# The last projection of a streaming encoder: begin with two tiles by column halves, weights in four buffers through ScalarE's queue

## What is computed

```python
h = rmsnorm(x, norm_w)
q, k, v, z_a, xbc, z_b, dt_raw, g_a, g_b = jnp.split(h @ w_in, split_points(SPLITS), axis=-1)
...
o_a = (attn * jax.nn.silu(z_a)) @ w_o_attn
o_b = y @ w_o_ssd
merged = jax.nn.sigmoid(g_a) * o_a + jax.nn.sigmoid(g_b) * o_b
x = x + (merged @ w_out).astype(x.dtype)
```

## Time and profile before

| | us |
|---|---|
| runs, median of 3 | 2492.91 (2492.88 to 2493.34) |
| profiled execution, its own time | 2494.7 |
| its span (first to last instruction) | 2493.0 |
| last stage, from SyncE's first issue to the end | 2269.0 to 2493.0 |
| TensorE matmul busy, whole span | 2349.9 (94%) |
| VectorE / ScalarE / GpSimd busy | 754.8 / 794.2 / 618.1 |
| mean granted TensorE clock | 0.970 |
| bytes moved by DMA | 250.10 MB, mean 100 GB/s |

### The profile page before, as it was taken

One profiled execution on the slowest core, in us unless ns is written; L12 is line 12 of the kernel. 1 busy time (PEld: TensorE's weight loads), 2 busy tenths in 40 slices (PEclk: granted clock), 3 DMA queues, 4 the chain that ended last, 5 costly groups with the idle time before them and its releaser, 6 DMA issues. The chain is left out here.

```text
span 2493.0 us, 35438 instructions
## 1 busy us (share of the span) xinstructions
PE 2349.9 (94%) x12807; PEld 2111.6 (85%) x12807; DVE 754.8 (30%) x1470; ACT 794.2 (32%) x1892; POOL 618.1 (25%) x547
## 2 busy tenths in 40 slices
PE   6999999999999999999999499999759999996999
PEld 5999999999999999999999478888547888774887
DVE  4211000024444000100000456555256566653221
ACT  5211112134444111221111355555235445432000
POOL 3110101101110111011010355555255665650000
PEclk9999999999999999999999699999969999997999
DMA  4411121211211212111118644444275656524432
GB/s 161 96 62 69 55 84 57 81 69 56 81 69 69 79 58 78 69 69 69 69 68 54 171 102 118 117 117 98 67 198 144 163 157 180 161 78 158 137 126 97
DMA packets 280002, 250.10 MB, mean 100 GB/s; under 512 B 74184, under 2 KB 257336, under 8 KB 272760
## 3 DMA queue, kind: packets, MB, share of 16 engines
q1 hardware_dynamic: 277832, 248.81, 34.8%
q10 hardware_dynamic: 2112, 0.53, 0.1%
HBM read 158.35 MB, written 90.95 MB: 100 GB/s over the span
## 5 line engine op out<-in xcount | busy, mean ns | idle before, releaser
L74 PE MATMUL acc<-h_hi,w_hi 128*128 128x424 f32 (+1 forms) x2280 | 811.0, 356 | 10.2 <-DVE h_lo L563 7.8
L75 PE MATMUL acc<-h_lo,w_hi 128*128 128x424 f32 (+1 forms) x2280 | 807.9, 354 | 0.0
L76 PE MATMUL acc<-h_hi,w_lo 128*128 128x424 f32 (+1 forms) x2280 | 807.9, 354 | 0.0
L74 PEld LDWEIGHTS acc<-h_hi,w_hi 128*128 128x128 f32 x2280 | 430.5, 189 | 24.5 <-DVE h_lo L563 8.6
L75 PEld LDWEIGHTS acc<-h_lo,w_hi 128*128 128x128 f32 x2280 | 431.1, 189 | 7.1
L76 PEld LDWEIGHTS acc<-h_hi,w_lo 128*128 128x128 f32 x2280 | 430.7, 189 | 7.1
L332 POOL TENSOR_TENSOR w_lo<-w_raw,w_hi 128x1024 fp32r<-128x1024 f32 x57 | 144.6, 2538 | 1130.6 <-ACT w_hi L374 1130.6
L399 ACT ACTIVATE row<-acc 128x424 f32<-128x424 f32 (+1 forms) x215 | 112.5, 523 | 825.3 <-PE acc L76 825.3
L599 DVE SCALAR_TENSOR_TENSOR conv_acc<-conv_in,conv_wb,conv_acc 128x424 f32<-128x424 f32 (+2 forms) x216 | 126.1, 585 | 380.9 <-ACT conv_acc L444 373.1
L74 PE MATMUL a_o_ps<-a_w_hi,a_at_hi 128*128 128x512 f32 (+1 forms) x272 | 117.7, 433 | 2.0 <-DVE a_branch L1294 2.0
L74 PE MATMUL s_o_ps<-s_w_hi,s_y_hi 128*128 128x512 f32 (+1 forms) x272 | 113.3, 416 | 5.9 <-ACT s_rows L1839 5.9
(11 more groups left out here) (215 smaller groups left out, 3049.6 us busy)
## 6 DMA issues: line engine op xcount, KB each, us to landing
proj<-row SPq DMA_DIRECT2D x56, 1056.0 KB, 4.0
w_raw<-in_w_in_dram SPq DMA_DIRECT2D x28, 1024.0 KB, 5.2
s_feat<-proj SPq DMA_DIRECT2D x16, 1280.0 KB, 7.9
s_acs_b<-acs_dram SPq DMA_DIRECT2D x16, 1024.0 KB, 7.3
a_q_diag<-proj SPq DMA_DIRECT2D x66, 128.0 KB, 4.4
a_z<-proj SPq DMA_DIRECT2D x16, 512.0 KB, 4.8
a_gate_t<-proj SPq DMA_DIRECT2D x16, 512.0 KB, 4.6
branch_rows<-a_branch SPq DMA_DIRECT2D x16, 512.0 KB, 3.2
```

Source lines behind the costliest of these rows:

```text
L74: pe.matmul(out, hi, whi, start=first, stop=False)
L75: pe.matmul(out, hi, wlo, start=False, stop=False)
L76: return pe.matmul(out, lo, whi, start=False, stop=last)
```

## The change

Only `project_out` changes.

- There are four raw weight buffers instead of two, and a semaphore for each. ScalarE's queue issues the four loads, before anything else on ScalarE, with no wait between them. SyncE issues rows 0, x 0, rows 1, x 1.
- ScalarE: four loads, high(0), high(1), four quarters' rounding, high(2), then as before from high(3). `high(2)` waits for three column halves' products instead of two.
- VectorE: low(0), low(1), four quarters' low parts, add_x(0), low(2), add_x(1), then as before.
- TensorE: turn(0), turn(1); wait for the low parts of both tiles; first column half of tile 0, of tile 1; second half of tile 0; turn(2); second half of tile 1; then step(2) as before, which begins with turn(3). The products' count for `add_x` follows that order.

The steps m = 0 and 1 are thus written out in this new order; step 2 and all later ones are unchanged. The diff, cut to its core:

```diff
-        w_raw = sb("w_raw", [P, 2, KT, D // 4])
+        w_raw = sb("w_raw", [P, 4, KT, D // 4])
...
-        w_loaded = [sem("w_loaded0"), sem("w_loaded1")]
+        w_loaded = [sem(f"w_loaded{q}") for q in range(4)]
...
         def steps(eng, step):
-            for m in range(3):
-                step(m, m % 2)
+            step(2, 0)
...
@@ sync
-            load_w(sp, 0)
             load(0, 0)
-            load_w(sp, 1)
             load(1, 1)
-            load_w(sp, 2)
-            load_w(sp, 3)
...
@@ scalar
+            def load_w(q):
+                act.dma_start(w_raw[:, q], io.w_out.rearrange("(k p) n -> p k n", p=P)[:, :, q * QUARTER:(q + 1) * QUARTER])\
+                    .then_inc(w_loaded[q], 16)
+            def high_w(q):
+                act.wait_ge(w_loaded[q], 16)
+                act.activation(w_hi[:, :, q * QUARTER:(q + 1) * QUARTER], w_raw[:, q], ACT.Copy)\
+                    .then_inc(S["w_hi_ready"], 1)
...
-                after(act, S["product_ready"], 2 * m - 2)
+                after(act, S["product_ready"], 3 if isinstance(m, int) and m == 2 else 2 * m - 2)
...
+            for q in range(4):
+                load_w(q)
             high(0, 0)
+            high(1, 1)
             for q in range(4):
-                high_w(act, q)
+                high_w(q)
+            high(2, 0)
...
@@ vector
+            def products(m, h):
+                if isinstance(m, int) and m < 2:
+                    return m + 1 + 2 * h
+                return 2 * m + h + 1
...
-                    dve.wait_ge(S["product_ready"], 2 * m + h + 1)
+                    dve.wait_ge(S["product_ready"], products(m, h))
...
             low(0, 0)
+            low(1, 1)
             for q in range(4):
-                low_w(dve, q)
+                low_w(q)
+            add_x(0, 0)
+            low(2, 0)
+            add_x(1, 1)
...
@@ tensor
             turn(0, 0)
+            turn(1, 1)
+            pe.wait_ge(S["lo_ready"], 4)
+            for h in range(2):
+                pe.wait_ge(S["w_lo_ready"], 2 * h + 2)
+                product(0, 0, h)
+                if h == 1:
+                    turn(2, 0)
+                product(1, 1, h)
```

More of the change, by code:

```diff
@@ L2204, in project_out @@
         stored = [sem("stored0"), sem("stored1")]
-        load_w, high_w, low_w = load_split_weights(io.w_out, w_raw, w_hi, w_lo, w_loaded,
-                                                   S["w_hi_ready"], S["w_lo_ready"])
+        QUARTER = D // 4
         block = ctx.enter_context(nc.Block())
         def steps(eng, step):
-            for m in range(3):
-                step(m, m % 2)
+            step(2, 0)
             with eng.Fori(0, (TILES - 4) // 2) as j:
@@ L2297, in low, with low_w @@
                         .then_inc(S["lo_ready"], 1)
+            def low_w(q):
+                n = slice(q * QUARTER, (q + 1) * QUARTER)
+                dve.wait_ge(w_loaded[q], 16)
+                dve.wait_ge(S["w_hi_ready"], q + 1)
+                dve.tensor_tensor(w_lo[:, :, n], w_raw[:, q], w_hi[:, :, n].bitcast(FP32), ALU.subtract)\
+                    .then_inc(S["w_lo_ready"], 1)
+            def products(m, h):
+                if isinstance(m, int) and m < 2:
+                    return m + 1 + 2 * h
+                return 2 * m + h + 1
             def add_x(m, slot):
@@ L2331, in turn, with product @@
                     mm.then_inc(S["turned"], 1)
+            def product(m, slot, h):
+                t = TokenTile(m)
+                n = slice(h * BANK, (h + 1) * BANK)
+                for k in range(KT):
+                    mm = split_matmul(pe, o_ps[0:t.n, slot, h, :], m_hi[:, slot, k, 0:t.n],
+                                      m_lo[:, slot, k, 0:t.n], w_hi[:, k, n], w_lo[:, k, n],
+                                      k == 0, k == KT - 1)
+                mm.then_inc(S["product_ready"], 1)
             pe.wait_ge(S["const"], 2)
             turn(0, 0)
+            turn(1, 1)
[6 more added lines that the diff above has]
+                product(1, 1, h)
             def step(m, slot):
@@ L2342, in step @@
                 for h in range(2):
-                    if isinstance(m, int) and m == 0:
-                        pe.wait_ge(S["w_lo_ready"], 2 * h + 2)
-                    n = slice(h * BANK, (h + 1) * BANK)
-                    for k in range(KT):
-                        mm = split_matmul(pe, o_ps[0:t.n, slot, h, :], m_hi[:, slot, k, 0:t.n],
-                                          m_lo[:, slot, k, 0:t.n], w_hi[:, k, n], w_lo[:, k, n],
-                                          k == 0, k == KT - 1)
-                    mm.then_inc(S["product_ready"], 1)
+                    product(m, slot, h)
             steps(pe, step)
```

## The result

The change makes the kernel slower: 2501.1 us (median of 7 runs, 2497.8 to 2505.5) against 2494.0 for the kernel before, also 7 runs. The ratio is 1.0029 with a 95% interval of 1.0019 to 1.0040, which is 7.1 us and clear of no change. The middle lies beyond the 0.2% that I took as the limit for slower, but the interval begins just inside it. I had forecast 2497.4 with a range up to 2500.6, and "within 0.2%" as the likeliest class. The sign of the working was right and its size was not.

A forecast was written before the change was run, and what follows sets the result against it. TensorE was taken to set the end, bound by a relay before its first product and one hole: +5.06 (later start) - 2.06 (hole) + 1.5 (rows of tile 3) = +4.5 us, giving a median of 2497.4, range 2494.3 to 2500.6.

The forecast's parts named there:

- hole of 2.06 us: TensorE's idle wait after tile 0's first half for the fourth weight quarter's split; forecast to go, -2.06 us.
- T: Moment when ScalarE is through its four load issues with tile 0 turned; forecast 2279.8, ends 2277.4 and 2282.4.
- in turn: Sharing rule for the two DMA queues: packets taken alternately; with 1570 weight packets moved, T = 2281.0.
- by bytes: Sharing rule for the two DMA queues: equal bytes each; with 1570 weight packets moved, T = 2278.6.
- The weights don't set it: Start of products: quarter two lands by 2284.4, before ScalarE comes to it at 2285.5.
- The second rival: ScalarE isn't held, issues some 0.7 us each; first product about 2288.2, +2.5 us in all, 2495.4; chance 0.20.
- From T to the first product: Turning, rounding and low parts of both tiles and weights before TensorE's first product: 10.4 us.
- the new wait: TensorE stands in `turn(3)` for rows of tile 3, whose load waits for `add_x(0)`; +1.5 us.
- The clock: TensorE's 1.2 GHz stretch after its first product, 5.26 us before; no change forecast, 0.8 us either way.
- The first rival: ScalarE's fourth issue held until the first two loads have left; T = 2282.4, +7.1 us, 2500.0; chance 0.22.
- The third rival: ScalarE held as forecast, but rows of tile 3 land in time for `turn(3)`; +3.0 us, 2495.9; chance 0.08.
- the fourth: Rival: first product no later than 2285.14 and no second wait; -2.1 us, 2490.8; chance 0.05.

The follow-up runs named there:

- Kernel 1: The kernel before with four raw weight buffers instead of two and nothing else; 2490.9 us, ratio to before 0.9986.
- kernel 2: The changed kernel with two buffers and SyncE's old order of loads, so only the tile order is new; 2498.8 us, ratio to before 1.0016.
- kernel 3: Kernel 1 with the four weight loads at the head of ScalarE's queue, old order of tiles; 2496.5 us, ratio to before 1.0008.
- kernel 5: The changed kernel with rows of tile 3 loaded ahead of x of tile 2 in SyncE's queue; 2498.9 us, ratio to before 1.0019.
- kernel 11: The changed kernel with SyncE silent after rows of tile 0 until all four weight loads have landed; one run, 2505.1 us.
- kernel 4: The changed kernel with weight loads three and four issued after the rounding of quarter two; 2496.0 us, ratio to before 1.0006.
- kernel 10: The changed kernel with the edits of kernel 4 and kernel 5 together; 2495.2 us, ratio to before 1.0002.
- kernel 12: The changed kernel with each 1 MB weight load in 512 packets of 2 KB; 2495.9 us, ratio to before 1.0010.
- kernel 9: The changed kernel measured once more, unaltered; 2500.1 us, ratio to before 1.0023.
- kernel 7: Kernel 1 with SyncE's loads in order of need: rows 0, w0, w1, rows 1, w2, w3, x last; 2490.6 us, ratio to before 0.9986.

## Why the prediction was right or wrong

**What bounds the stage: right.** TensorE's hole of 2.06 us was all that there was to gain. It went, in every kernel with four buffers, and no second-half wait took its place. Kernel 1 shows its worth: 2.0 us at `turn(3)`. The order removes it without more buffers too (kernel 2).

**ScalarE held in its own issues: right in kind, short in size.** This is the step that failed. I put the moment T at which ScalarE is free at 10.8 us into the stage (2279.8), and it was 12.54. That is 1.7 of the 2.0 us by which the start was missed. T was the middle of two readings, and there were two mistakes in it.

- I averaged two rules of sharing, "in turn" (2281.0) and "by bytes" (2278.6), since no row of before told them apart. The trace after speaks for the first: 538 packets of one queue to 583 of the other, over 6.5 us. By "in turn" alone T would have been 12.0 us into the stage. A rule of the Trainium skill, which I had not weighed, points the same way: DMA: Bandwidth & Descriptors, section "Queues, rings and completion order", says that an engine goes round-robin between the queues it has work for, switching only between packets, where a packet of that page holds several of the rows that the profile counts. The trace agrees from 2274.5 on (538 to 583), but not in the 2.6 us before that, with 666 packets of ScalarE's queue to 90 of SyncE's. For T that stretch changes little, because SyncE's loads had all moved by the release either way.
- I let both queues move from 1.1 us into the stage. ScalarE's moved only from 2.6 us, 1.5 later. In that time SyncE's queue moved 79 packets, 0.32 MB, worth 0.8 us at the forecast's rate, and 39 packets fewer than I reckoned with had to move, 0.1 us. That leaves 0.6 us, an estimate from these counts, for the 0.54 between 12.0 and 12.54.

The count of packets at the release came out right, 1531 for 1570, and that is partly luck: kernels 3 and 5 were released with 1218 and 1254 moved, and kernel 11 with 1502 but with a third issue that fits no such count.

**"The weights don't set it": right here, and a close second.** In the changed kernel ScalarE rounds all four quarters without a wait. But quarter two landed at 15.6 us, the 15.4 of my bound and 4.4 later than before, and such a landing alone keeps the first product at 19.3 to 19.6, over 3 us late (kernels 3, 4, 10 and 12). The second rival had this price, +3.06 at the first product without any hold, and kernel 4 measured 3.3: that rival was wrong on the hold and right on what stays without it.

The section that I had cited, "Issuing engines are not separate DMA queues" of the Trainium skill's DMA: Bandwidth & Descriptors, calls the time to initiate a transfer "usually small relative to the DMA itself". Here it was 12.54 us of an engine's time, where the loads take 13.9 us and more from issue to landing, and it was on the path. With 4 KB packets (2.10 us for all four) the sentence holds.

**From T to the first product: right.** Forecast 10.4, measured 10.63 (2292.48 less 2281.85). The missing 0.2 is ahead of `turn(1)`, 1.51 us after the release instead of 1.29: two hand-overs between engines that I had not counted.

**The hole and the new wait: right.** -2.06 forecast, and it is gone. +1.5 forecast in `turn(3)`, measured 1.38, and 1.23 and 1.56 in kernels 9 and 4. Kernel 5 shows that it is the late issue of the rows.

**The clock: forecast none, 0.8 either way.** The stretch at 1.2 GHz was 4.80 us, not 5.26. Over all kernels it was 3.1 to 6.0 us, which at the forecast's 0.46 us per us is 1.0 us less to 0.3 us more than before, so 0.8 either way was a little narrow. The change of stretch here is 0.2 us gained. From the first product to `turn(3)` it took 26.58 us against 27.56: -0.98, where -2.06 + 1.38 and the clock's -0.2 make -0.9.

**The sum.** Forecast +5.06 - 2.06 + 1.5 = +4.5. Measured +7.03 - 0.98 = +6.05 at `turn(3)`, and 0.3 from the stage's start. The first term was 1.97 us too small, and the others came out 0.42 better than I had put them. In the medians it is 7.1 us with an interval of 4.7 to 10; the traces, one execution of each, show 6.4. The forecast of 2497.4 missed 2501.1 by 3.7: 1.9 by these terms and the stage's start, 1.0 because the kernel before had a median of 2494.0 over 7 runs and not 2492.9 as over the first 3, and 0.8 is left to the scatter between executions.

**The class: probably wrong.** I had given 0.64 to a change within 0.2%. The two ratios are 1.0029 and 1.0023, and both intervals reach below 1.002. I had written that slower begins once T passes 2280.3, that is 11.3 us into the stage. T was 12.5 by that count. The first rival had T = 2282.4, 13.4 us in, and +7.1 in all. The measured T lies nearer to it (0.9) than to the forecast (1.7), and so does the time. But its mechanism, that the fourth issue is held until the first two loads have left, isn't what happened: 2048 packets would have had to move, and 1531 had. The other reason that it gave, one generator of packets shared by both queues, is neither shown nor refuted, as said above. The third rival falls by the wait of 1.38 us. The second rival, short issues, is refuted by the trace for the changed kernel, and the fourth by the first product at 23.17 instead of 16.14.

**What the prediction didn't see.** It gave the order no price beyond the work of the second tile, and that was right for the changed kernel only because SyncE's queue is short in it. Kernel 2 shows the same order at +5.5 with SyncE's old queue. Nor did it ask whether the one gain could be had without the rest. Kernel 1 answers that: 2.0 us at `turn(3)` for two more buffers.

## What to carry to other kernels

A DMA command is work of the engine that issues it: count the packets, not the bytes, and place long runs of short-row loads on a queue whose engine has nothing to compute, or issue only as many as are needed first. Then ask when the load that the start needs will land: with the hold mended, the landing in the other queue still cost 3.2 to 3.3 us here (kernels 10 and 4). Before a step is doubled ahead of a critical product, look for what the doubled step waits for and where that stands in its queue. And when a change joins several edits, ask which of them removes the idle time at the least price: here the extra buffers alone did it at none, and what the other two cost at the start was more than the 2.06 us.

## What the runs showed of the hardware that I had not expected

- Four loads of 1 MB in 1 KB packets hold ScalarE 12.54 and 12.84 us beside SyncE's traffic, 11.17 and 11.27 in two kernels close to it, and 7.26 almost without traffic; in 2 KB packets 4.44; in 4 KB packets 2.10. The first two issues are short (1.06 us for both in kernel 4, 0.43 and 0.59 in the changed kernel).
- The fourth issue took 4.9 us in four kernels, while 425 to 690 packets of its queue moved. A count of outstanding packets doesn't explain that.
- Two queues shared the engines about packet for packet once both were well under way: 538 packets, mostly of 4 KB, against 583 of 1 KB in 6.5 us. In the 2.6 us before that it was 90 to 666, and no run shows why. The queue with short rows gets a quarter of the bytes (0.58 of 2.56 MB), so moving a load to a second queue can slow it down.
- A queue that is issued to at the same moment as another can start later: ScalarE's first packet moved 2.6 us after its issue, SyncE's within about 1 us.
- The granted clock rose 3.1 us after the first product in kernels 2, 5 and 7, 4.8 in the changed kernel and in 1 and 3, 5.3 in the kernel before and 6.0 in kernel 12. Kernel 5 and the changed kernel have the same code on TensorE and stood the same 7.18 us before their first product, and differ by 1.7 us. So a lead of up to 1.3 us (an estimate, 0.46 us per us over the 2.9 us between the ends) in one execution can be the clock and not the kernel.
